# Two triangular inversions merged into one VectorE stream, and modulation products moved into the attention stage

## The reference

```python
mod_lat = (silu_c @ ada_w[l] + ada_b[l])[:, None, :]      # ada_w[l]: 1024 x 6144
sh1, sc1, gt1, sh2, sc2, gt2 = jnp.split(mod_lat, 6, axis=-1)
h = modulate(rms_norm(x, norm_g[l, 0]), sh1, sc1)
...
m = jnp.where(strict, jnp.einsum('nbhid,nbhjd->nbhij', kb, kc) * decay, 0.0)
tmat = lax.linalg.triangular_solve(eye + m, ..., lower=True, unit_diagonal=True)
```

## Time and profile before

| what | us |
|---|---|
| median of three runs | 1442.46 |
| lowest, highest | 1442.0, 1447.43 |
| the profiled execution | 1445.46 |
| its span, first to last instruction | 1443.7 |
| PE busy | 1261.5 (87%) |
| DVE busy | 679.3 (47%) |
| ACT busy | 563.5 (39%) |
| POOL busy | 232.0 (16%) |

### The profile page before, as it was taken

How to read it: one execution, slowest core, us unless ns; L and a number is a source line. 1 busy time by engine, 2 the same in 40 slices (tenths; PEclk the granted TensorE clock), 3 DMA queues, 4 the chain that set the end, 5 groups by cost and what they waited for, 6 DMA issues and landing times.

```text
span 1443.7 us, 19692 instructions
## 1 busy us (share of the span) xinstructions
PE 1261.5 (87%) x7965; PEld 1025.7 (71%) x7965; DVE 679.3 (47%) x1023; ACT 563.5 (39%) x971; POOL 232.0 (16%) x233
## 2 busy tenths in 40 slices
PE   5699978889599999999999589967758978899996
PEld 3377745668277777777878358866648967899996
DVE  2443276553643332323222554459974465545444
ACT  2322255553432222222222346563355534444442
POOL 1121320000411111001000310029403231211101
PEclk9899999999799999999999779888976998999998
DMA  7655411223135555555433112222100214466561
GB/s 273 185 166 159 143 63 59 60 59 88 29 117 172 167 161 168 167 171 168 124 106 88 44 44 74 59 73 72 46 0 18 74 30 117 118 180 185 172 184 40
DMA packets 239142, 159.64 MB, mean 111 GB/s; under 512 B 14523, under 2 KB 213581, under 8 KB 239053
## 3 DMA queue, kind: packets, MB, share of 16 engines
q1 hardware_dynamic: 238272, 158.10, 37.0%
q10 hardware_dynamic: 780, 0.29, 0.1%
HBM read 157.32 MB, written 1.05 MB: 110 GB/s over the span
## 4 chain that ended last, share of the span: by engine, by line
PE 74%; DVE 14%; ACT 6%; issue 2%; DMA 2%; POOL 1%; ACTq 0%; SPq 0%; DVEq 0%; POOLq 0%
PE bank L1339 55%; PE bank L1327 3%; PE bank L1489 2%; PE bank L1466 2%; PE bank L1378 2%; DVE w_lo L1746 2%; DVE h_lo L1793 1%; DVE xT L1816 1%; PE bank L760 1%; PE bank L1309 1%; DVE conv_out L1033 1%; DVE q_fm L1033 1%; PE bank L1474 1%; DVE h_hi L1792 1%; DVE outer L1181 1%
## 5 line engine op out<-in xcount | busy, mean ns | idle before, releaser
L1339 PE MATMUL bank<-h_hi,w_hi 128*128 128x512 f32 (+2 forms) x1240 | 448.9, 362 | 77.7 <-DVE w_lo L1746 33.8
L1339 PE MATMUL bank<-h_lo,w_hi 128*128 128x512 f32 (+2 forms) x1240 | 438.2, 353 | 0.0
L1339 PE MATMUL bank<-h_hi,w_lo 128*128 128x512 f32 (+2 forms) x1240 | 437.2, 353 | 0.0
L1746 DVE TENSOR_TENSOR w_lo<-w_raw,w_hi 128x1024 fp32r<-128x1024 f32 (+1 forms) x203 | 252.3, 1244 | 338.1 <-ACT w_hi L1550 337.4
L1339 PEld LDWEIGHTS bank<-h_hi,w_hi 128*128 128x128 f32 (+1 forms) x1240 | 244.3, 197 | 138.2 <-issue 97.3
L1339 PEld LDWEIGHTS bank<-h_hi,w_lo 128*128 128x128 f32 (+1 forms) x1240 | 244.7, 197 | 30.7 <-issue 1.5
L1339 PEld LDWEIGHTS bank<-h_lo,w_hi 128*128 128x128 f32 (+1 forms) x1240 | 245.3, 198 | 26.7 <-issue 0.5
L1550 ACT ACTIVATE w_hi<-w_raw 128x1024 fp32r<-128x1024 f32 (+1 forms) x203 | 209.3, 1036 | 109.2 <-PE bank L1339 93.0
L1339 PE MATMUL bank<-act_hi,w_hi 128*128 128x512 f32 (+1 forms) x352 | 119.3, 339 | 0.0
L1339 PE MATMUL bank<-act_hi,w_lo 128*128 128x512 f32 (+1 forms) x352 | 119.0, 338 | 0.0
L1339 PE MATMUL bank<-act_lo,w_hi 128*128 128x512 f32 (+1 forms) x352 | 118.8, 338 | 0.0
(11 more groups left out here) (257 smaller groups left out, 1500.8 us busy)
## 6 DMA issues: line engine op xcount, KB each, us to landing
w_raw<-in_ada_w SPq DMA_DIRECT2D x96, 512.0 KB, 6.1
w_raw<-in_ffn_w_gate_up SPq DMA_DIRECT2D x88, 512.0 KB, 3.8
w_raw<-in_ffn_w_down SPq DMA_DIRECT2D x32, 512.0 KB, 4.0
w_raw<-in_gdn_w_in SPq DMA_DIRECT2D x32, 512.0 KB, 4.0
w_raw<-in_attn_w_in SPq DMA_DIRECT2D x14, 512.0 KB, 4.0
w_raw<-in_ffn_w_down SPq DMA_DIRECT2D x16, 384.0 KB, 3.4
w_raw<-in_attn_w_out SPq DMA_DIRECT2D x8, 512.0 KB, 4.8
w_raw<-in_gdn_w_out SPq DMA_DIRECT2D x8, 512.0 KB, 5.7
```

What stands on the lines that cost most here:

```text
L1339: m = nc.tensor.matmul(dst, stationary(a, k), moving(b, k), start=(first and k == kk[0] and a == b == 0), stop=(last and k == kk[-1] and a ...
L1746: nc.vector.tensor_tensor(w_lo[where[key] % N_RAW][:, 0:tiles, 0:w], raw_slot(key)[:, 0:tiles, 0:w], w_hi[m % N_SPLIT][:, 0:tiles, 0:w].bi ...
```

## The change

**Modulation.** `ada_after` no longer places anything in the gate and down stages. In attention a pair is multiplied in every unit n with n % 3 not zero, 31 pairs from unit 1 to unit 46 instead of seven. The list of chunks, and so the order of loads, follows.

**Substitution.** Both directions' blocks lie in one tile and are solved by DVE in one stream of 30 steps with twice the elements, spread over projection steps 16 to 29. The factor on the blocks is multiplied in for both while they are put out (`block_scale`). GpSimd zeroes the other triangle of both blocks and sets the diagonals before the solve instead of after it, and it masks the decay tiles, now with affine selects, before that. The inverses are put out at steps 30 and 31, into weight slots 2 and 3; ACT copies the first back at step 31 and the second behind Z32, which now reads the inverses themselves. The value evacuations move from DVE to ACT as four scaled copies each. ACT waits for the last solve step before it writes z of head 6, since the products lie there. GpSimd clears the upper blocks before the query multiplies.

```diff
+ATT_PAIR = {n: n - n // 3 - 1 for n in range(len(ATT_UNITS)) if n % 3}
-    if phase == "att" and step % 6 == 5 and step // 6 < 7:
-        return pair(34, step // 6)
-    if phase == "gate0" and step % 2:
-        return pair(48, step // 2)
-    if phase == "down0" and step in (1, 3):
-        return pair(92, step // 2)
+    if phase == "att" and step % 3 and ATT_PAIR[step] < 31:
+        return pair(34, ATT_PAIR[step])
...
-        INVERSE_AT = 27
+        INVERSE_AT = 30
-        SOLVE_AT = {16 + m: [2 * m + 1, 2 * m + 2] for m in range(15)}
+        SOLVE_AT = {16 + m: [j for j in range(1, BLOCK - 1) if (j - 1) * 14 // 30 == m] for m in range(14)}
...
-            jobs = [("inverse", 1), ("kt", 0), ("kt", 1), ("vt", GH - 1), ("kt", 2), ("kt", 3), ("turn", 0)]
-            jobs += [("Z32", half) for half in range(2)] + [("turn", 1)]
+            jobs = [("kt", 0), ("kt", 1), ("vt", GH - 1), ("kt", 2), ("kt", 3), ("turn", 0)]
+            jobs += [("Z32", half) for half in range(2)] + [("turn", 1), ("inverse", 1)]
...
+        def values_out(act, h):
+            job = ("vt", h)
+            wait_product(act, job)
+            if h == 0:
+                act.wait_ge(key_norms, 1)
+            for c in range(CHUNKS):
+                last = nc.scalar.activation(v_tok[:, h, c, :], bank(job)[:, tokens(c)], ACT.Copy,
+                                            scale=key_norm[:, c, h:h + 1])
+            release(last, job)
...
+                        if h == GH - 2:
+                            act.wait_ge(steps_done, 1)
                         release(nc.scalar.activation(z_fm[:, h, :], bank(key)[:, CTX:T], ACT.Silu), key)
...
+            def solve_step(j):
+                below, known = slice(j + 1, BLOCK), slice(0, j)
+                shape = [P, 2, BLOCK - 1 - j, j]
+                product = outer[:, 0:2 * shape[2] * j].rearrange("p (d i k) -> p d i k", d=2, k=j)
+                link(nc.vector.tensor_tensor(product, blocks[:, :, below, j].unsqueeze(3).to_broadcast(shape),
+                                             blocks[:, :, j, known].unsqueeze(2).to_broadcast(shape), ALU.mult))
+                ins = nc.vector.tensor_tensor(blocks[:, :, below, known], blocks[:, :, below, known], product, ALU.add)
...
-            pool.wait_ge(blocks_in, 1)
-            solve_begin(nc.gpsimd, link, 0)
-            for n in range(1, BLOCK - 1):
-                solve_step(nc.gpsimd, link, 0, n)
-            pool.wait_ge(steps_done, 1)
-            solve_end(pool, link, 0)
-            for c in range(LAT_CHUNK, CHUNKS):
-                mask_decays(c)
-            pool.wait_ge(steps_done, 2)
-            solve_end(pool, link, 1)
-            pool.wait_ge(blocks_solved, 2)
+            for c in range(LAT_CHUNK, CHUNKS):
+                for hq in range(2):
+                    wait_evacuated(pool, ("G", c, hq))
+                mask_decays(c)
+            pool.wait_ge(blocks_in, 1)
+            link(nc.gpsimd.affine_select(blocks, blocks, [[0, 2], [1, BLOCK], [-1, BLOCK]], ALU.is_gt, 0.0, base=0,
+                                         channel_multiplier=0))
+            nc.gpsimd.memset(blocks.rearrange("p d i j -> p d (i j)")[:, :, 0:BLOCK * BLOCK:BLOCK + 1],
+                             1.0).then_inc(blocks_masked, 1)
             clear(False)
+            clear(True)
             decay_queries(0)
             decay_queries(1)
-            pool.wait_ge(q_decayed, 4)
-            clear(True)
```

More of the change, by code:

```diff
@@ L186, in stream @@
         for n in range(2 * FT):
-            out += [("gate", layer, n)] + [("ada", a) for a in ada_after(f"gate{layer}", n)]
+            out += [("gate", layer, n)]
         for m in range(KT):
             out += [("down", layer, m, part) for part in range(3)]
-            out += [("ada", a) for a in ada_after(f"down{layer}", m)]
     return out
@@ L862, in gdn_scalar @@
                     nc.scalar.activation(key_norm, key_norm, ACT.Exp, scale=0.5).then_inc(key_norms, 1)
-                if n == INVERSE_AT:
+                h = turned_at(n - 1)
+                if h is not None:
+                    values_out(act, h)
+                if n == INVERSE_AT + 1:
                     inverse_back(act, 0)
@@ L963, in blocks_out @@
                 dve.wait_ge(diagonals_in, d + 1)
-                return nc.vector.transpose(blocks[d].rearrange("p i j -> p j i"), diagonals[d].rearrange("p u j -> p j u"))
+                return nc.vector.transpose(blocks[:, d].rearrange("p i j -> p j i"),
+                                           diagonals[d].rearrange("p u j -> p j u"))
             def block_scale(d):
                 link(nc.vector.transpose(neg_d2b[d], beta_g[:, :, d * GH:(d + 1) * GH]))
-                nc.vector.scalar_tensor_tensor(out=neg_d2b[d], in0=neg_d2b[d], scalar=-1.0, in1=inv_b, op0=ALU.mult,
-                                               op1=ALU.mult).then_inc(blocks_in, 1)
@@ L982, in turn_out @@
-            def turn_out(d):
+                link(nc.vector.scalar_tensor_tensor(out=neg_d2b[d], in0=neg_d2b[d], scalar=-1.0, in1=inv_b,
+                                                    op0=ALU.mult, op1=ALU.mult))
+                return nc.vector.tensor_tensor(blocks[:, d], blocks[:, d],
+                                               neg_d2b[d].unsqueeze(2 if d else 1).to_broadcast([P, BLOCK, BLOCK]),
+                                               ALU.mult)
+            def solve_step(j):
[5 more added lines that the diff above has]
+                ins = nc.vector.tensor_tensor(blocks[:, :, below, known], blocks[:, :, below, known], product, ALU.add)
+                if j == BLOCK - 2:
+                    ins.then_inc(steps_done, 1)
+                else:
+                    link(ins)
@@ new lines, in inverse_out, with turn_scale @@
+            def inverse_out(d):
+                dve.wait_ge(steps_done, 1)
+                wait_product(dve, ("gdn",) + GDN_STEPS[LAST - 5 + d])
+                way = "p i j -> p j i" if d else "p j i -> p j i"
+                nc.vector.transpose(inverses[d].rearrange("p u j -> p j u"),
+                                    blocks[:, d].rearrange(way)).then_inc(inverse_in, 1)
+            def turn_scale(d):
+                dve.wait_ge(inverse_in, d + 1)
+                nc.vector.tensor_tensor(blocks[:, d], blocks[:, d],
+                                        neg_d2b[d].unsqueeze(1 if d else 2).to_broadcast([P, BLOCK, BLOCK]),
+                                        ALU.mult).then_inc(blocks_scaled, 1)
@@ L984, in turn_out @@
+            def turn_out(d):
+                if d == 0:
+                    wait_product(dve, ("gdn", "z", GH - 1))
                 dve.wait_ge(blocks_scaled, d + 1)
-                nc.vector.transpose(turned_blocks[d].rearrange("p u i -> p i u"), blocks[d]).then_inc(turned_in, 1)
+                way = "p i j -> p i j" if d else "p j i -> p i j"
+                nc.vector.transpose(turned_blocks[d].rearrange("p u i -> p i u"),
+                                    blocks[:, d].rearrange(way)).then_inc(turned_in, 1)
@@ L1416, in ffn @@
                     done_at[("y", i, m)] = jobs[0]
-                    ada(ada_after(f"down{layer}", m))
             pe.wait_ge(tables_in, 16)
```

104 lines of the change are left out of this document (28 added, 76 removed).

## The result

The changed kernel takes 1404.84 us (median of 4 runs, 1403.31 to 1406.29) against 1443.2 for the kernel before on the same chip (4 runs): a ratio of 0.9729, 95% interval 0.9706 to 0.9752. Two later measurements gave 0.9714 (0.9694 to 0.9733) and 0.9734 (0.9716 to 0.9753).

The account below looks back on a forecast made before the run. Taken as bounds: TensorE in the gate stage, mixed in attention (TensorE dense in units 24 to 43), DVE in mid-DeltaNet. 1445.46 - 8.8 (modulation) - 10.3 (substitution) = 1426.4, less 3.0: 1423 us, range 1406 to 1438.

Parts of the forecast that it names:

- The likeliest case: Whole kernel: modulation gives -8.8 us and substitution -10.3, so 1423 us; chance 0.48.
- The fourth rival: Attention and DeltaNet: early pairs fill the holes wholly and the solve saturates, -18 and -20, 1404 to 1406 us; chance 0.13.
- Two pairs cost 2.73 us: Gate and down stages: two modulation pairs with one fold, 1.365 us each, so removing 24 pairs takes off 32.8 us.
- I take half: Attention units 0 to 23: of 14.5 us for 12 added pairs, half hides in TensorE's idle time, leaving 7.5 us.
- The last pair and the landing: End of attention: 1.2 us for the last pair and closing fold, 2 for a late output-projection chunk at unit 44.
- Rival 3: Attention: the loads set the pace, at 225 GB/s 65 us instead of 54, 11 more, total 1434; chance 0.10.
- The chosen step: DeltaNet: all of DVE's slower instructions are put down to GpSimd working beside it, -18.1 us.
- DVE's one idle stretch: DeltaNet: 4.13 us before a w_lo, ended by ACT; moving the first inverse's copies behind all weight splits gives -4 us.
- The selects at zero: DeltaNet: five selects on GpSimd, 1.4 us for 1024 elements, priced at 0 for DVE.
- Rival 2: DeltaNet: the GpSimd selects hold DVE, 8.4 us at most, taken as 5, total 1428; chance 0.07.
- Rival 1: DeltaNet: TensorE's pace eats the solve's gain, the substitution half gives 1 or 2 us instead of 10, total 1432; chance 0.16.
- Rival 5: Units with a pair: DVE's copy binds TensorE, 2.9 us a pair, total 1469; decides from 2.1 us a pair; chance 0.06.

Follow-up runs that it names:

- e3: Kernel before with four modulation chunks after every fourth gate projection instead of two after every second: ratio 0.9965 to the kernel before, gate stage 276.0 instead of 279.7 us.
- e4: Changed kernel with its last two modulation pairs put back into the down stage, behind tiles 1 and 3: 1404.07 us, ratio 0.9742 to the kernel before.
- e5: Changed kernel with 60 extra GpSimd multiplications of 240 elements, reading and writing SBUF, beside DVE's substitution: 1423.51 us, ratio 0.9873 to the kernel before.
- e6: Changed kernel with 120 extra GpSimd fills of 240 elements, only writing SBUF, beside DVE's substitution: 1402.55 us, ratio 0.9719 to the kernel before.
- e13: Kernel before with GpSimd doing only the last of its 30 substitution steps, first inverse left unsolved: 1433.17 us, ratio 0.9931.
- e11: Kernel before with ACT's four copies of the first inverse moved behind the last projection step: 1444.15 us, ratio 1.0006.
- the candidate with both edits: Changed kernel with key copies ahead of the second inverse's, and attention's last two pairs after gate projection 3: 1399.45, then 1399.3 us.
- e8: Changed kernel with the eight scaled value copies put back from ACT to DVE: 1406.31 us, ratio 0.9752 to the kernel before.

## Why the prediction was wrong

The direction was right, the size was half: 19 us of 38 are missing from the sum. The step that failed is the pricing of the modulation pairs, -8.8 us forecast and -23.3 measured. A pair in the gate or down stage was priced by the chain's pieces alone, 1.365 us; it cost 1.58 in the gate stage and 3.7 in the down stage. And the pairs put into attention were taken as half hidden with a wait for a late landing behind them, 24.0 us; they cost 18.9. These sizes make 14.5 of the 19 us. The second step is DVE's waits in the DeltaNet stage, -2 forecast and -7.0 measured, where one wait wasn't seen and one cause was missed. The likeliest case (0.48) erred to the same side in all of these (points 1 to 3, 5 and 7 below). The fourth rival (0.13) names the measured time, 1404 to 1406, in part by luck: its halves are -18 and -20, the measured ones -23.3 and -16.4.

1. **"Two pairs cost 2.73 us" in the gate stage (-30.0; measured -34.8).** The chain's small pieces are not all that a pair takes. With a start in them two projections take 11.11 us, without one 10.88 after the change. 22 x 0.23 = 5.1 covers the whole error of 4.8. e3 shows it by itself: 0.24 us inside the projections and 0.11 inside the chunks for each interruption saved.
2. **"Two pairs the down stage", at the same 1.365 (-2.7; measured -7.4).** A size again: e4 puts 5.65 us back for two pairs; the closing fold waits for DVE's copy with nothing behind it. The other 1.7 us of the 7.4 are low clock behind this wait: 61.56 us for the last 264 matmuls, where e3 has 60.01. Four of the five profiles with the old lists have it (126.8 or 126.9 us for the stage), e3 and e4 don't (125.2 and 125.1).
3. **"I take half" of twelve early pairs (+7.5; measured +5.1, +1.8 in the third profile, whose clock fell elsewhere: 11.19 + 70.14 - 79.54, and +3.4 between the means).** The holes filled for the most part. The argument that the hole moves along with DVE's copy fell: waits of the transposes for the probabilities, over both lines of DVE that end them, went from 13.8 us (9.6 of them in the earlier trace rows) to 3.7; 1.7 us of waits for DVE's copy came instead. Units 4 to 23 come out at 70.1 or 70.2 us in thirteen profiles with the pairs and scatter from 65.5 to 70.4 in five without. The stream with holes had falls of the clock there (0.94 and 0.87 in the earlier trace rows), the filled one had none (1.00 from 199.2 on). That filling is what kept the clock up is the plain reading; no run tests it by itself.
4. **The dense stretch, 11 x 1.21 = 13.3 (measured 12.0).** The price was right and the count one too high: units 24 to 43 hold 13 pairs after the change and 3 before, 10 added at 1.20 each. The eleventh lies in unit 44.
5. **The last pair and the landing (+3.2; measured +1.8 for two pairs).** The landing wait of 2 us did not come: ACT's first split at unit 44 waits 0.7 us, TensorE's own waits for raw chunks are 1.2 us in the whole run, 261 GB/s were carried. Rival 3, with its 225 GB/s that no run shows, is out.
6. **DVE's sum (-12.5; measured 97.85 - 84.58 = -13.3).** Right: w_lo -2.6 (forecast -2.6), products and sums 27.5 to 30.2, +2.7 (+2.6), query convolutions -6.5 (-7.7), values -4.8 (-4.8), and the value convolutions -1.4 (not priced). The chosen step, that all of it is GpSimd, is borne out by e5, e6 and e13 (with GpSimd only writing, in e6, the means stay short).
7. **The waits around it (-4 + 2; measured -7.0).** Idle stretches of 4.21, 4.13 and 3.20 us became 2.80 and 1.76. Both forecast pieces were right: the 4.13 of the earlier trace rows are gone, and z of head 6 costs 1.76. What failed is "DVE's one idle stretch": the prediction had not seen the 3.20 at 1066.67, since its groups ended at 1048.6, and took the first, 4.21, as given; they shrank by 3.20 and 1.41. e11 shows that moving the copies alone brings nothing in the old places, since the values of head 6 then wait 4.69 us for them. The 3.20 is the projection at the lower clock. In the changed kernel TensorE waits 1.78 us before this projection instead of 8.22, its granted clock is 1.00 over the last 46 us before the second inverse, and the wait is gone; which edit does it was not isolated.
8. **ACT's 11.0 us from the first inverse to Z32.** Measured 1037.69 - 1026.70 = 10.99; the chain's rows are the pieces of that sum:

```profile
1026.74 1.06 ACT gram L785
...
1031.85 1.03 ACT v_tok L795 x4
...
1032.90 1.28 ACT L1546
...
1034.19 1.09 ACT k_tok L881 x2
...
1035.28 1.03 ACT v_tok L795 x4
1036.31 0.98 ACT k_tok L881 x2
...
1037.69 1.88 PE bank L641 x123
```

9. **The second inverse's copies before T32 (+4.3; measured 16.2 - 10.1 = +6.1).** Right in kind: four copies of 1.06 from 1047.20 on, then 2.07 for the keys. The stretch is 14.0 to 16.7 us in the profiles with this order and 9.9 to 10.6 in those of the old one. With the keys first it is 12.0 and 11.1, in the candidate with both edits 9.6 and 11.2. The last term, -1 for the earlier clearing of the upper blocks, can't be seen: from T32 to the scan it is 30.2 us before and 31.4 after.
10. **The selects at zero.** Four mask selects (2.16 and 2.15 us a pair) fell into DVE's idle time. The one over both blocks did not. GpSimd, then DVE:

```profile
952.33 3.29 POOL L1246 TENSOR_SCALAR_AFFINE_SELECT blocks<-blocks 128x2048 f32<-128x2048 f32 x1 [18.35 <-DVE blocks L984]
```

```profile
952.18 1.22 DVE L1736 TENSOR_TENSOR w_lo<-w_raw,w_hi 128x1024 fp32r<-128x1024 f32 x1
953.31 3.61 DVE L1071 SCALAR_TENSOR_TENSOR q_fm<-conv_in,conv_cols,q_fm 128x256 f32<-128x256 f32 x3
```

The w_lo that began first kept its usual 1.22 us. The first of the three convolutions took 2.57 instead of 0.48 and ended at 955.88, just behind the select (955.62); the three together took 3.61 instead of 1.52, 2.1 us more. The select's 3.29 hold a wait too: from the end of w_lo, 953.40, to its own are 2.22, twice the 1.08 of a mask select, and in e8, where a value copy of 0.68 comes in place of that w_lo, it takes 2.37. Rival 2's lock is real, its 5 us were 2.

Rival 1 (TensorE's pace) fell: the stretch became 20.4 us shorter, and the granted clock was 0.93 on the mean where it had been 0.83. Rival 5 fell: 12 us for 10 pairs in the dense stretch, 1.2 each against the 2.1 from which it would decide.

## What to carry to other kernels

Small work in the middle of a full stream of matmuls costs its own length and a restart (here 0.23 to 0.33 us each); read that from the length per matmul with and without interruptions, not from the chain's pieces. A last piece that needs another engine's copy costs that wait as well. Moved into a stage where the engine has holes, such work can be nearly free. When an engine is found busy throughout a stretch, look at its waits up to the very end of that stretch: idle time was here a third of what the stretch gained (7.0 of 20.4 us). And before a copy is moved out of the way, look who waits for it in the code: in the kernel before, the wait only came back at the next instruction that writes to that memory.

## What was not expected of the hardware

- Wherever the granted clock is 1.00 the same attention units take the same time in profile after profile: units 24 to 43 take 52.70 to 52.72 us in all profiles with the new lists. Between executions of one kernel the shorter ones have the higher mean clock (key copies first, second measurement: 1396.63 us at 0.943, 1402.98 at 0.936). In unit 2 the low level (1.2 GHz) behind TensorE's wait of 1.95 us cost 3.4 us; ahead of it, on the first scores, it only shortened the wait.
- GpSimd's writes (120 fills, 36 us) left the means of w_lo, the convolutions and the solve steps as they were, to a nanosecond or two; reads of 57.7 us took 23.4 us from it.
- A select over 128x1024 fp32 on GpSimd took 1.08 us in pairs while DVE was mostly idle, and 1.38 and 1.44 beside DVE's work in the kernel before. Over 128x2048 it took 3.29, of which about 1.07 was waiting for a DVE instruction that had begun before it. Each side waits for the other: a DVE convolution of 0.48 us behind it took 2.57.
